# One single chunk and five pairs in each feed-forward in place of three and four, and a one-row bias table

## The chip, the cores and the metric

One NeuronCore of one Trainium2 chip runs the whole program. The metric is device time in microseconds, the median of three runs. Engines are named as in the profile: PE (TensorE), DVE (VectorE), ACT (ScalarE), POOL (GpSimd) and SP (SyncE); SP and POOL issue most transfers.

## The reference

All sizes: 256 tokens, width 1024, float32. The first block has two layers. Layer 0 is a Conformer convolution, layer 1 a causal differential attention of 8 heads with a T5 relative bias. Behind each stands the feed-forward and a gated projection of side features. A second block of three branches follows. What the change touches:

```python
def swiglu(x, w_gate, w_up, w_down):
    return (jax.nn.silu(x @ w_gate) * (x @ w_up)) @ w_down      # width 2816

u = rms_norm(h, ffn_norm_g[i])                                  # once a layer
h = h + swiglu(u, ffn_w_gate[i], ffn_w_up[i], ffn_w_down[i])

bias = jnp.transpose(rel_bias[t5_bucket(dist)], (2, 0, 1))      # dist = q_pos - k_pos
logits = jnp.where(dist >= 0, logits + bias, -jnp.inf)
```

## The kernel before, in words

**Arithmetic.** Each float32 matrix product is made of three passes of reduced-precision matmuls: with x_hi and w_hi, x_lo and w_hi, x_hi and w_lo. `w_hi` is a rounded copy of a weight piece, made by ACT (`feed`, line 1297), and `w_lo` what is left of it, made by DVE (`feed`, line 1857), of a few pieces by POOL (line 1069). A weight piece is 128 x 2048 numbers, 1 MB. PE needs w_hi from the first pass and w_lo from the third.

**Stream.** All weights form one list of operations (`STREAM`, `FFN_ORDER`). Each takes its place in three slots of `w_hi` and `w_lo` in turn, so that w_hi of an operation can be made when PE has left the one three places back (`w_used`). SP loads the plain pieces in the order of the list into four buffers `raw` (line 385) and asks for one when w_lo of the piece four back has been made.

**Feed-forward.** The gate and up columns are cut in 11 chunks of 256 and 256. A *single* chunk is two operations of 24 matmuls (`token_chunk`, line 441). A *pair* of chunks is computed by Strassen's scheme in Winograd's form: with tokens and depth halved, seven products of 12 matmuls (`product`, line 564) in place of eight. B11, B21 and B22 use plain weight pieces. T1, T2, T3 and T4 use sums of pieces, kept in three slots `sums` in the arena. POOL's queue loads them and adds to them by accumulating transfers: T1 is a load of B11 (line 1164, for the first pair 1115) and an accumulation of B12 (line 1106). T4 is a load of B12 (line 1168, first pair 1150) and an accumulation of B22 (line 1109). T2 is T1 + B22, added by DVE (line 1994, `second_sum`). T3 is an accumulation of B21 upon T2 (line 1156). The sums of the tokens' side (`q_hi`, `q_lo`) are made once a layer by DVE and ACT while chunk 0 runs.

Out of the products p1 to p7 come four quarters: chunk one or two, tokens 0 or 1. ACT copies three of them out of PSUM (`c_11`, `c_22`, `c_12`), DVE adds the others, ACT takes the silu and DVE multiplies (`gated`, lines 1361 and 1979). The semaphore `hidden` counts the quarters in the order of `MADE`. A finished hidden chunk is transposed by PE (`hidden_job`, line 603) and split by ACT and DVE (lines 1353 and 1972). Then a *down* operation (24 matmuls) adds its product to four banks. The order of PE, of ACT's and DVE's work and of the queues is written out by hand: a down piece and the transposing of another chunk lie between the products of a pair.

**Bias.** A row of 384 numbers for each head, with the distance falling, is written to DRAM 128 times for each head (line 1177), and read back with a row step of 383, which shifts each partition by one (lines 1181 and 1183). `masked` (line 2267) adds it to the logits.

## Time and profile before

| | |
|---|---|
| median of three runs | 1002.41 us (1000.92 to 1003.13) |
| the profiled execution's own time | 1003.63 us |
| its span | 1001.6 us |
| PE busy | 988.1 us (99%) |
| DVE, ACT, POOL busy | 775.3, 609.2, 153.6 us |
| DMA | 242.01 MB, 242 GB/s over the span |
| SP's queue q1, POOL's queue q0 | 43.8% and 28.2% of the sixteen engines' span |

A matmul's end is modelled and the next one starts before it, so what one costs is read from the starts. The feed-forwards lie from 109.7 us to 288 us and from 429.4 us to 605 us.

### The profile page before, as it was taken

Reading aid. Unit: us, or ns where it says so; the run is one execution under the profiler, and the core shown is the slowest. Engines: PE = TensorE matmul, PEld = TensorE weight load, DVE = VectorE, ACT = ScalarE, POOL = GpSimd, SP = SyncE. Lnnn points to the kernel's source line nnn. Section 1 sums busy time; section 2 is a strip of 40 time slices with the busy share of each in tenths; the row PEclk is TensorE's granted clock in tenths of the full one; section 3 lists DMA queues with packets and bytes.
Section 4 is the critical chain, followed back from the end, with each engine's and each line's share of the span. In section 5 each row is a group of like instructions: output and inputs, shape, how many; then the busy total and the mean of one; then the engine's idle time right before and its main releaser. Section 6 shows DMA issues by size and latency. Waiting matters only on the chain.

```text
span 1001.6 us, 13597 instructions
## 1 busy us (share of the span) xinstructions
PE 988.1 (99%) x5350; PEld 835.5 (83%) x5350; DVE 775.3 (77%) x909; ACT 609.2 (61%) x722; POOL 153.6 (15%) x150
## 2 busy tenths in 40 slices
PE   8999999999999999999999999999999999999997
PEld 8977888888778888788888888788888889999886
DVE  6996888879567666787988857876877788777874
ACT  6437567657376668666676646754857574444733
POOL 4992101101030320111111002100100010000000
PEclk9999999999999999999999999999999999999999
DMA  8862899999784632779999864577789898545631
GB/s 324 256 217 90 274 298 324 334 300 305 209 292 161 238 128 85 256 264 300 331 343 338 256 218 167 189 256 280 262 258 341 237 311 299 186 169 179 220 126 43
DMA packets 37726, 242.01 MB, mean 242 GB/s; under 512 B 4504, under 2 KB 7064, under 8 KB 9760
## 3 DMA queue, kind: packets, MB, share of 16 engines
q1 hardware_dynamic: 23904, 167.26, 43.8%
q0 software_dynamic: 10736, 70.71, 28.2%
q10 hardware_dynamic: 3024, 3.18, 1.3%
q8 instruction: 43, 0.70, 0.3%
q14 instruction: 19, 0.16, 0.0%
HBM read 237.91 MB, written 3.21 MB: 241 GB/s over the span
## 4 chain that ended last, share of the span: by engine, by line
PE 80%; DVE 8%; DMA 6%; issue 3%; ACT 1%; POOL 0%; SPq 0%; ACTq 0%; POOLq 0%; DVEq 0%
PE bank L441 45%; PE bank L564 18%; DVE bank L2160 4%; PE bank L427 4%; PE bank L429 4%; PE bank L428 4%; DMA raw<-in_ws 4%; DMA arena<-in_ws 3%; PE bank L478 2%; DVE w_lo L1857 2%; PE bank L603 1%; PE bank L847 0%; DMA u_scr<-arena 0%; PE bank L944 0%; PE bank L977 0%
## 5 line engine op out<-in xcount | busy, mean ns | idle before, releaser
L1857 DVE TENSOR_TENSOR w_lo<-raw,w_hi 128x2048 fp32r<-128x2048 f32 x145 | 332.8, 2303 | 84.0 <-ACT w_hi L1297 83.7
L1297 ACT ACTIVATE w_hi<-raw 128x2048 fp32r<-128x2048 f32 x156 | 298.2, 1912 | 107.9 <-PE bank L441 71.3
L1297 ACT ACTIVATE w_hi<-arena 128x2048 fp32r<-128x2048 f32 x48 | 92.4, 1924 | 57.2 <-PE bank L441 21.0
L441 PE MATMUL bank<-w_hi,x_hi 128*128 128x512 f32 x416 | 115.0, 398 | 0.2
L1857 DVE TENSOR_TENSOR w_lo<-arena,w_hi 128x2048 fp32r<-128x2048 f32 x48 | 109.2, 2285 | 5.3 <-ACT w_hi L1297 5.2
L441 PE MATMUL bank<-w_lo,x_hi 128*128 128x512 f32 x416 | 111.5, 390 | 0.0
L441 PE MATMUL bank<-w_hi,x_lo 128*128 128x512 f32 x416 | 111.5, 390 | 0.0
L441 PE MATMUL bank<-w_hi,z_hi 128*128 128x512 f32 x320 | 94.2, 394 | 0.3 <-DVE z_lo L1972 0.3
L441 PE MATMUL bank<-w_lo,z_hi 128*128 128x512 f32 x320 | 92.9, 390 | 0.1
L441 PE MATMUL bank<-w_hi,z_lo 128*128 128x512 f32 x320 | 92.9, 390 | 0.0
L441 PEld LDWEIGHTS bank<-w_hi,x_lo 128*128 128x128 f32 x416 | 78.1, 188 | 16.8
L441 PEld LDWEIGHTS bank<-w_lo,x_hi 128*128 128x128 f32 x416 | 78.1, 188 | 16.5
L441 PEld LDWEIGHTS bank<-w_hi,x_hi 128*128 128x128 f32 x416 | 75.2, 188 | 16.3 <-issue 1.7
L428 PE MATMUL bank<-x_lo,w_hi 128*128 128x256 f32 x256 | 72.4, 283 | 0.0
L429 PE MATMUL bank<-x_hi,w_lo 128*128 128x256 f32 x256 | 72.4, 283 | 0.0
L427 PE MATMUL bank<-x_hi,w_hi 128*128 128x256 f32 x256 | 72.4, 283 | 0.0
L441 PEld LDWEIGHTS bank<-w_lo,z_hi 128*128 128x128 f32 x320 | 60.0, 188 | 13.1 <-DVE w_lo L1857 0.5
L441 PEld LDWEIGHTS bank<-w_hi,z_lo 128*128 128x128 f32 x320 | 60.1, 188 | 12.7
L441 PEld LDWEIGHTS bank<-w_hi,z_hi 128*128 128x128 f32 x320 | 58.8, 188 | 12.5 <-DVE z_lo L1972 0.7
L1069 POOL TENSOR_TENSOR w_lo<-raw,w_hi 128x2048 fp32r<-128x2048 f32 x11 | 50.7, 4615 | 110.9 <-ACT w_hi L1297 110.8
L564 PE MATMUL bank<-w_hi,q_hi 128*128 128x512 f32 x192 | 52.9, 397 | 1.0 <-ACT arena L1751 1.0
L564 PE MATMUL bank<-w_lo,q_hi 128*128 128x512 f32 x192 | 51.6, 391 | 0.0
(292 smaller groups left out, 1592.3 us busy)
## 6 DMA issues: line engine op xcount, KB each, us to landing
raw<-in_ws SPq DMA_DIRECT2D x156, 1024.0 KB, 7.3
arena<-in_ws POOLq DMA_DIRECT2D x60, 1024.0 KB, 11.4
arena<-u_scr ACTq DMA_DIRECT2D x16, 142.0 KB, 4.9
arena<-in_rows POOLq DMA_DIRECT2D x2, 1024.0 KB, 6.6
toep<-bias_row POOLq DMA_DIRECT2D x1, 1536.0 KB, 44.7
h<-in_x_tok SPq DMA_DIRECT2D x2, 512.0 KB, 4.0
raw<-in_ws SPq DMA_DIRECT2D x2, 512.0 KB, 8.0
arena<-in_rows POOLq DMA_DIRECT2D x2, 512.0 KB, 7.5
```

The costliest lines, as they stand in the source:

```text
L427: pe.matmul(dst, s_hi, m_hi, start=first, stop=False)
L428: pe.matmul(dst, s_hi, m_lo, start=False, stop=False)
L429: return pe.matmul(dst, s_lo, m_hi, start=False, stop=last)
L441: ins = pe.matmul(dst, tok(a_part, k, t), w_part[:, s, c], start=first and j == 0 and i == 0, stop=last and j == 2 and i == len(ks) - 1)
L478: ins = pe.transpose(banks[b][:, k * P:(k + 1) * P], src[:, k * P:(k + 1) * P], ident[:, :])
L564: ins = pe.matmul(banks[b][:, :], a_part[:, k, :], w_part[:, o % SPLIT, k * 512:(k + 1) * 512], start=start and j == 0 and k == 0, stop=j ...
L603: ins = pe.transpose(banks[t_bank][:, k * SEQ + t * P:k * SEQ + (t + 1) * P], hids[i % 3][:, t, k * P:(k + 1) * P], ident[:, :])
L1069: pool.tensor_tensor(w_lo[:, g % SPLIT, :], operand(g), w_hi[:, g % SPLIT, :].bitcast(F32), ALU.subtract).then_inc(S("lo_pool"), 1)
L1297: act.activation(w_hi[:, g % SPLIT, :], operand(g), ACT.Copy).then_inc(hi_done, 1)
L1857: dve.tensor_tensor(w_lo[:, g % SPLIT, :], operand(g), w_hi[:, g % SPLIT, :].bitcast(F32), ALU.subtract).then_inc(lo_done, 1)
L2160: ins = dve.scalar_tensor_tensor(out=y_odd[:, f % 2, :] if tap == TAPS - 2 else sums[c], in0=shifted, scalar=w, in1=sums[c], op0=ALU.mult, ...
```

## The change

Chunk 1 and chunk 10, single before, become part of pairs: (1, 2), (3, 4), (5, 6), (7, 8), (9, 10) behind the single chunk 0. B21 moves to the second place of a pair. The first and the last pair have one down piece within them, behind T4; the others have two. Three down pieces (7, 10, 9) stand at the end of a layer. The quarter (one, 0) is gated first, before T2's turn is over, and DVE gates the last quarter before it makes w_lo of the next pair. POOL's queue adds T3 of the first pair before it loads T1 of the second. PE's banks alternate between two arrangements. The bias row has the distance rising and is written once for each head, 383 numbers; one load reads it with a step of one number from partition to partition, and `masked` reads it backwards.

```diff
-STEPS = (0, 1, (2, 3), (4, 5), (6, 7), (8, 9), 10)
-PAIRS = [s for s in STEPS if isinstance(s, tuple)]
+STEPS = (0, (1, 2), (3, 4), (5, 6), (7, 8), (9, 10))
+PAIRS = STEPS[1:]
 NPAIR = len(PAIRS)
-WITHIN = {(2, 3): (0, 1), (4, 5): (3, 2), (6, 7): (5, 4), (8, 9): (7, 6)}
-BEHIND = {10: (9, 8, 10)}
-
-TURNED = {(2, 3): (1, None), (4, 5): (3, 2), (6, 7): (5, 4), (8, 9): (7, 6), 1: (0,), 10: (9,)}
-LAST_DOWN = BEHIND[10][-1]
-
-FFN_ORDER = []
-for _step in STEPS:
-    if isinstance(_step, tuple):
-        FFN_ORDER += [(_step, "B11"), (_step, "T1"), (_step, "T2"), (_step, "B22"), ("down", WITHIN[_step][0]),
-                      (_step, "B21"), (_step, "T4"), ("down", WITHIN[_step][1]), (_step, "T3")]
-    else:
-        FFN_ORDER += [("gu", _step, 0), ("gu", _step, 1)] + [("down", i) for i in BEHIND.get(_step, ())]
+WITHIN = {(1, 2): (0,), (3, 4): (2, 1), (5, 6): (4, 3), (7, 8): (6, 5), (9, 10): (8,)}
+BEHIND = (7, 10, 9)
+
+TURNED = {(1, 2): (None, 0), (3, 4): (2, 1), (5, 6): (4, 3), (7, 8): (6, 5), (9, 10): (8, 7)}
+LAST_DOWN = BEHIND[-1]
+
+FFN_ORDER = [("gu", 0, 0), ("gu", 0, 1)]
+for _p in PAIRS:
+    FFN_ORDER += [(_p, "B11"), (_p, "B21"), (_p, "T1"), (_p, "T2"), (_p, "B22")]
+    FFN_ORDER += [("down", i) for i in WITHIN[_p][:-1]] + [(_p, "T4"), ("down", WITHIN[_p][-1]), (_p, "T3")]
+FFN_ORDER += [("down", i) for i in BEHIND]
...
 for _layer in range(2):
-    for _step in STEPS:
-        if isinstance(_step, tuple):
-            MADE += [(_layer, _step[1], 0), (_layer, _step[0], 0), (_layer, _step[1], 1), (_layer, _step[0], 1)]
-        else:
-            MADE += [(_layer, _step, t) for t in range(TT)]
+    MADE += [(_layer, 0, t) for t in range(TT)]
+    for _one, _two in PAIRS:
+        MADE += [(_layer, _one, 0), (_layer, _two, 0), (_layer, _two, 1), (_layer, _one, 1)]
...
                     one, two = p
                     n = pair_no(layer, p)
-                    b1, b4, b2 = [(1 + PAIRS.index(p) + j) % 3 for j in range(3)]
+                    b1, b4, b2 = ((2, 1, 0), (1, 2, 0))[PAIRS.index(p) % 2]
                     turned, within = TURNED[p], WITHIN[p]
                     product(("p1", n), ffn_at(layer, p, "B11"), *of_x(0, t0), b1, True, (S("c_11"), 2 * n - 1))
-                    hidden_job(turned[0])
-                    if n == NPAIR * layer + 1:
+                    if turned[0] is not None:
+                        hidden_job(turned[0])
+                    product(("p2", n), ffn_at(layer, p, "B21"), *of_x(1, t0), b2, True, (S("c_11"), 2 * n))
+                    if p == PAIRS[0]:
                         pe.wait_ge(S("q_lo"), layer + 1)
                     product(("p5", n), ffn_at(layer, p, "T1"), *of_q(0), b4, True, (S("c_22"), 2 * n - 1))
                     product(("p6", n), ffn_at(layer, p, "T2"), *of_q(1), b1, False, (S("c_12"), 2 * n - 1))
-                    if turned[1] is not None:
-                        hidden_job(turned[1])
+                    for i in turned[1:]:
+                        hidden_job(i)
                     product(("p3", n), ffn_at(layer, p, "B22"), *of_q(2), b4, False, (S("c_12"), 2 * n))
-                    down(within[0])
-                    product(("p2", n), ffn_at(layer, p, "B21"), *of_x(1, t0), b2, True, (S("c_11"), 2 * n))
+                    for i in within[:-1]:
+                        down(i)
                     product(("p7", n), ffn_at(layer, p, "T4"), *of_q(3), b1, False, (S("c_22"), 2 * n))
-                    down(within[1])
+                    down(within[-1])
                     product(("p4", n), ffn_at(layer, p, "T3"), *of_x(1, t1), b1, False, (S("hidden"), MADE_NO[layer, one, 1]))
-                for step in STEPS:
-                    if isinstance(step, tuple):
-                        pair(step)
-                    else:
-                        single(step)
+                token_chunk(("gu", layer, 0), g0, x_hi, x_lo, ready=ready_from(m),
+                            release=lambda t: (S("hidden"), MADE_NO[layer, 0, t]), hooks=later(m, 1))
+                for p in PAIRS:
+                    pair(p)
+                for j, i in enumerate(BEHIND):
+                    if j + 1 < len(BEHIND):
+                        hidden_job(BEHIND[j + 1])
+                    down(i)
             def ple(layer, m):
                 g0 = G[f"ple{layer}"]
...
                 for before, p in zip(PAIRS, PAIRS[1:]):
                     lo_ready(pool, ffn_at(layer, before, "T1"))
                     sum_there(pool, layer, before, "T2")
+                    if before == PAIRS[0]:
+                        third_sum(layer, before)
                     pool.dma_start(sums[:, 0, :], ws[PIECE_OF[ffn_at(layer, p, "B11")]]).then_inc(S("t1_in"), 16)
-                    third_sum(layer, before)
+                    if before != PAIRS[0]:
+                        third_sum(layer, before)
                     second_part("T1", layer, p)
                     lo_ready(pool, ffn_at(layer, before, "T4"))
                     pool.dma_start(sums[:, 2, :], ws[B12_ROW[layer, p]]).then_inc(S("t4_in"), 16)
@@ -1174,14 +1165,11 @@
             weight_sums(0)
             pool.wait_ge(S("bias_row"), 1)
             pool.wait_ge(S("bias_masked"), 1)
-            pool.dma_start(toep, bias_row[:, :].unsqueeze(1).to_broadcast([HEADS, P, 384])).then_inc(S("toep_out"), 16)
+            pool.dma_start(toep, bias_row[:, 0:383]).then_inc(S("toep_out"), 16)
             low(G["ple0"] + 1)
             h_factor(1)
             pool.wait_ge(S("toep_out"), 16)
-            pool.dma_start(toep_t[:, :, 0:SEQ], bass.AP(toep.tensor, P - 1, [[383, P], [P * 384, HEADS], [1, SEQ]])) \
-                .then_inc(S("ld_toep"), 16)
-            pool.dma_start(toep_t[:, :, SEQ:384], bass.AP(toep.tensor, 2 * P - 1, [[383, P], [P * 384, HEADS], [1, P]])) \
-                .then_inc(S("ld_toep"), 16)
+            pool.dma_start(toep_t, bass.AP(toep.tensor, 0, [[1, P], [383, HEADS], [1, SEQ]])).then_inc(S("ld_toep"), 16)
...
+                def first():
+
+                    ahead(g0)
+                    act.wait_ge(S("r_done"), m + 1)
                     for t in range(TT):
-                        bank, _ = take(act, (("gu", layer, i), t))
-                        gated(i, t, bank[:, 0:256])
-                        if i == 0 and t == 0:
+                        bank, _ = take(act, (("gu", layer, 0), t))
+                        gated(0, t, bank[:, 0:256])
+                        if t == 0:
                             act.wait_ge(S("q_sums"), layer + 1)
                             act.activation(q_hi.rearrange("p i k c -> p (i k c)"),
                                            q_f32.rearrange("p i k c -> p (i k c)"), ACT.Copy).then_inc(S("q_hi"), 1)
-                            ahead(g + 1)
-                    behind = BEHIND.get(i, ())
-                    for j, k in enumerate(behind):
-                        if j + 1 < len(behind):
-                            hidden_hi(behind[j + 1])
-                        ahead(ffn_at(layer, "down", k))
+                            ahead(g0 + 1)
...
-                    ahead(o)
                     while left:
                         left.pop()()
+                    ahead(o)
                     bank, _ = take(act, ("p1", n))
                     act.activation(c_11, bank[:, :], ACT.Copy).then_inc(S("c_11"), 1)
                     ahead(o + 1)
-                    hidden_hi(turned[0])
+                    if turned[0] is not None:
+                        hidden_hi(turned[0])
+                    ahead(o + 2)
+                    act.wait_ge(S("c_11"), 2 * n)
+                    gated(one, 0, c_11[:, 0:256])
                     bank, _ = take(act, ("p5", n))
                     act.activation(c_22, bank[:, :], ACT.Copy).then_inc(S("c_22"), 1)
-                    ahead(o + 2)
-                    if turned[1] is not None:
-                        hidden_hi(turned[1])
+                    ahead(o + 3)
+                    for i in turned[1:]:
+                        hidden_hi(i)
                     bank, _ = take(act, ("p6", n))
                     act.activation(c_12, bank[:, :], ACT.Copy).then_inc(S("c_12"), 1)
-                    ahead(o + 3)
                     ahead(o + 4)
+                    ahead(o + 5)
                     act.wait_ge(S("c_12"), 2 * n)
                     gated(two, 0, c_12[:, 0:256])
-                    ahead(o + 5)
-                    ahead(o + 6)
-                    act.wait_ge(S("c_11"), 2 * n)
-                    gated(one, 0, c_11[:, 0:256])
+                    ahead(ffn_at(layer, p, "T4"))
                     act.wait_ge(S("c_22"), 2 * n)
                     gated(two, 1, c_22[:, 0:256])
-                    ahead(o + 7)
-                    ahead(o + 8)
+                    ahead(ffn_at(layer, p, "T3"))
...
-                for step in STEPS:
-                    if isinstance(step, tuple):
-                        pair(step)
-                    else:
-                        single(step)
+                first()
+                for p in PAIRS:
+                    pair(p)
+                left.pop()()
+                for j, i in enumerate(BEHIND):
+                    if j + 1 < len(BEHIND):
+                        hidden_hi(BEHIND[j + 1])
+                    ahead(ffn_at(layer, "down", i))
...
+                def first():
+
+                    feed(g0 + 1)
+                    input_sums(m)
+                    ahead(g0)
...
+                        if t == 0:
                             input_lo(m)
-                            ahead(g + 1)
-                    behind = BEHIND.get(i, ())
-                    for j, k in enumerate(behind):
-                        if j + 1 < len(behind):
-                            hidden_lo(behind[j + 1])
-                        ahead(ffn_at(layer, "down", k))
+                            ahead(g0 + 1)
+                    second_sum(PAIRS[0])
                 def pair(p):
                     one, two = p
                     n, o = pair_no(layer, p), ffn_at(layer, p, "B11")
                     turned = TURNED[p]
-                    ahead(o)
                     while left:
                         left.pop()()
-                    hidden_lo(turned[0])
+                    ahead(o)
+                    if turned[0] is not None:
+                        hidden_lo(turned[0])
                     ahead(o + 1)
+                    p_2, _ = take(dve, ("p2", n))
+                    dve.wait_ge(S("c_11"), 2 * n - 1)
+                    dve.tensor_tensor(c_11, p_2[:, :], c_11, ALU.add).then_inc(S("c_11"), 1)
                     ahead(o + 2)
-                    if turned[1] is not None:
-                        hidden_lo(turned[1])
+                    dve.wait_ge(S("c_11"), 2 * n)
+                    gated(one, 0, c_11[:, 256:512])
+                    for i in turned[1:]:
+                        hidden_lo(i)
+                    ahead(o + 3)
                     p_53, _ = take(dve, ("p3", n))
                     dve.wait_ge(S("c_12"), 2 * n - 1)
                     dve.tensor_tensor(c_12, p_53[:, :], c_12, ALU.subtract).then_inc(S("c_12"), 1)
-                    ahead(o + 3)
+                    ahead(o + 4)
                     dve.wait_ge(S("c_12"), 2 * n)
                     gated(two, 0, c_12[:, 256:512])
-                    ahead(o + 4)
-                    ahead(o + 5)
-                    p_2, _ = take(dve, ("p2", n))
-                    dve.wait_ge(S("c_11"), 2 * n - 1)
-                    dve.tensor_tensor(c_11, p_2[:, :], c_11, ALU.add).then_inc(S("c_11"), 1)
+                    ahead(ffn_at(layer, p, "T4") - 1)
                     u_3, _ = take(dve, ("p7", n))
                     dve.wait_ge(S("c_22"), 2 * n - 1)
                     dve.tensor_tensor(c_22, c_22, u_3[:, :], ALU.subtract).then_inc(S("c_22"), 1)
-                    dve.wait_ge(S("c_11"), 2 * n)
-                    gated(one, 0, c_11[:, 256:512])
-                    ahead(o + 6)
+                    ahead(ffn_at(layer, p, "T4"))
                     dve.wait_ge(S("c_22"), 2 * n)
                     gated(two, 1, c_22[:, 256:512])
-                    ahead(o + 7)
+                    ahead(ffn_at(layer, p, "T3"))
                     if p != PAIRS[-1]:
                         second_sum(PAIRS[PAIRS.index(p) + 1])
-                    ahead(o + 8)
...
+                first()
+                for p in PAIRS:
+                    pair(p)
+                left.pop()()
+                for j, i in enumerate(BEHIND):
+                    if j + 1 < len(BEHIND):
+                        hidden_lo(BEHIND[j + 1])
+                    ahead(ffn_at(layer, "down", i))
...
-            act.activation(bias_row[:, 0:SEQ], bank[0:HEADS, 0:SEQ], ACT.Copy).then_inc(S("bias_row"), 1)
+            act.activation(bias_row[:, P - 1:P - 1 + SEQ], bank[0:HEADS, 0:SEQ], ACT.Copy).then_inc(S("bias_row"), 1)
...
-            pool.memset(bias_row[:, SEQ:384], NEG).then_inc(S("bias_masked"), 1)
+            pool.memset(bias_row[:, 0:P - 1], NEG).then_inc(S("bias_masked"), 1)
...
-                        ins = dve.tensor_tensor_reduce(v[:, lo:lo + w], bank[:, k0:k0 + w], toep_t[:, hd, k0:k0 + w],
+                        ins = dve.tensor_tensor_reduce(v[:, lo:lo + w], bank[:, k0:k0 + w], toep_t[:, hd, w - 1::-1] if w < SEQ else toep_t[:, hd, ::-1],
...
-            dve.wait_ge(S("ld_toep"), 32)
+            dve.wait_ge(S("ld_toep"), 16)
...
-    dist = np.arange(SEQ - 1, -1, -1)
+    dist = np.arange(SEQ)
...
-    toep = nc.dram_tensor("toep", (HEADS, P, 384), F32).ap()
+    toep = nc.dram_tensor("toep", (HEADS, 383), F32).ap()
```

## Rows read from the trace of the kernel before

**Rows 1.** The page: busy time, share and instructions; DMA share in 40 slices.

```profile
PE 988.1 (99%) x5350; PEld 835.5 (83%) x5350; DVE 775.3 (77%) x909; ACT 609.2 (61%) x722; POOL 153.6 (15%) x150
...
DMA  8862899999784632779999864577789898545631
```

**Rows 2.** Waits of PE: line, releaser, us in total, times, longest.

```profile
PE bank L603 <- DVE z_lo L1972: 1.0, 1, 1.0
```

**Rows 3.** Windows: length, busy time of each engine, clock, DMA share, GB/s.

```profile
109.60:132.80 23.20, 23.20 (x110) 19.27 (x109) 22.12 (x19) 12.91 (x13) 3.84 (x5) 1.00 0.83 274
...
191.40:222.40 31.00, 31.00 (x143) 25.61 (x142) 24.40 (x18) 20.91 (x18) 3.71 (x5) 1.00 1.03 318
...
510.60:541.50 30.90, 30.90 (x142) 25.54 (x141) 26.91 (x20) 21.20 (x18) 3.62 (x5) 1.00 1.02 324
```

**Rows 4.** Windows of 5 us: accumulating pieces alone, then plain ones alone.

```profile
140.00:145.00 5.00, 5.00 (x24) 4.14 (x23) 4.43 (x3) 4.31 (x4) 0.86 (x1) 1.00 0.92 192
...
235.00:240.00 5.00, 4.93 (x22) 3.72 (x21) 5.00 (x5) 4.29 (x5) 0.00 (x0) 1.00 1.02 203
155.00:160.00 5.00, 5.00 (x24) 4.14 (x23) 4.69 (x5) 2.63 (x3) 0.00 (x0) 1.00 1.00 424
475.00:480.00 5.00, 5.00 (x24) 4.13 (x23) 5.00 (x5) 2.32 (x2) 0.00 (x0) 1.00 1.02 429
```

**Rows 5.** Timeline of PE (start us, us): chunk 0's end, T2, B22, two pairs' starts.

```profile
121.47 1.07 PE L441 MATMUL bank<-w_hi,x_hi 128*128 128x512 f32 x4
...
138.79 1.07 PE L564 MATMUL bank<-w_hi,q_hi 128*128 128x512 f32 x4
...
141.51 1.07 PE L564 MATMUL bank<-w_hi,q_hi 128*128 128x512 f32 x4
...
163.27 1.07 PE L564 MATMUL bank<-w_hi,x_hi 128*128 128x512 f32 x4
...
194.19 0.62 PE L564 MATMUL bank<-w_hi,x_hi 128*128 128x512 f32 x2
```

**Rows 6.** Timeline of DVE: behind chunk 0 in layer 0, a sum of quarters, layer 1.

```profile
125.74 0.48 DVE L1979 SCALAR_TENSOR_TENSOR arena<-bank,st,arena 128x256 f32<-128x256 f32 x1
126.14 2.28 DVE L1994 TENSOR_TENSOR arena<-arena,raw 128x2048 f32<-128x2048 f32 x1
128.34 2.28 DVE L1857 TENSOR_TENSOR w_lo<-raw,w_hi 128x2048 fp32r<-128x2048 f32 x1
...
144.43 0.69 DVE L2038 TENSOR_TENSOR arena<-bank,arena 128x512 f32<-128x512 f32 x1 [0.57 <-PE bank L564]
...
448.02 2.28 DVE L1857 TENSOR_TENSOR w_lo<-raw,w_hi 128x2048 fp32r<-128x2048 f32 x1
```

**Rows 7.** Timeline of POOL (first load of T4) and ACT (w_hi of T3, T4, T4).

```profile
118.67 0.64 POOL L1150 DMA_DIRECT2D arena<-in_ws  x1 [4.77 <-DVE arena L1956]
...
438.38 0.62 POOL L1150 DMA_DIRECT2D arena<-in_ws  x1 [4.78 <-DVE arena L1956]
...
218.04 1.92 ACT L1297 ACTIVATE w_hi<-arena 128x2048 fp32r<-128x2048 f32 x1 [4.36 <-DMA arena<-in_ws]
...
238.82 1.93 ACT L1297 ACTIVATE w_hi<-arena 128x2048 fp32r<-128x2048 f32 x1 [0.71 <-DMA arena<-in_ws]
...
557.39 1.93 ACT L1297 ACTIVATE w_hi<-arena 128x2048 fp32r<-128x2048 f32 x1 [0.42 <-DMA arena<-in_ws]
```

**Rows 8.** T1(8,9): w_lo, third pass; bias table: transfer, ACT's waits behind it, reductions.

```profile
227.87 4.49 DVE L1857 TENSOR_TENSOR w_lo<-arena,w_hi 128x2048 fp32r<-128x2048 f32 x2
...
230.21 1.20 PE L564 MATMUL bank<-w_lo,q_hi 128*128 128x512 f32 x4
...
toep<-bias_row POOLq DMA_DIRECT2D x1, 1536.0 KB, 44.7
...
ACT w_hi L1297 <- DMA raw<-in_ws: 18.1, 6, 5.3
...
L2267 DVE CUSTOM_DVE_ANT_0 arena<-bank,arena 128x256 f32<-128x256 f32 x16 | 6.7, 421 | 5.6 <-PE bank L848 5.5
```

47 lines of the change are left out of this document (3 added, 44 removed).

## The prediction

> **What bounds the kernel now.** I read the page's busy shares and slices first. TensorE is busy 988.1 us of a 1001.6 us span, 99% [rows 1]. Next the waits of TensorE: few, and the largest in a feed-forward is 1.0 us, once, in layer 0: the transposes of a hidden chunk wait for VectorE's z_lo [rows 2]. So a TensorE instruction taken away is worth its full price, as long as its feeders stay ahead. Then I read the DMA line of the page: it reaches 9 exactly in the two feed-forwards (and in stretches of the second block). Cut at the starts of pairs, the sixteen DMA engines are full there: share 1.03 and 318 GB/s in the third pair of layer 0, 1.02 and 324 GB/s in that of layer 1, while the stretch over chunks 0 and 1 has 0.83 [rows 3]. The kernel is thus at two limits at once in the pairs, TensorE and the DMA engines, and the second one is hidden only by work that was fetched ahead.
>
> How close is shown by ScalarE, which makes w_hi from what arrives: in layer 0 it waits 4.36 us for T3 of the third pair and 0.71 us for T4 of the fourth (arena: the POOL queue's sums) [rows 7]. It gets away with it because w_hi is made up to three operations ahead. But TensorE's third pass of T1(8,9), which needs w_lo, starts at 230.21; w_lo was ready at 227.87 + 2.28 = 230.15, so the slack is gone [rows 6, 8]. (Which operation a w_hi or w_lo row belongs to is counted by its place in the stream.)
>
> **The change: TensorE.** Twelve matmuls make one product: T2 starts at 138.79 and B22 at 141.51, 2.72 us [rows 5]. One half of a single chunk and a down piece have 24 matmuls of the same shape each, 5.44 us. Two single chunks (10.88 us each) become one pair of seven products (19.04 us): 2.72 us saved a layer, 5.44 us in all. Transposes and down pieces keep their number.
>
> **The first pair, VectorE.** Up to the second sum VectorE does the same as before in the same order, and it is full (22.1 of 23.2 us, [rows 3]): gating 125.74, second sum 126.14, next w_lo 128.34 to 130.62 [rows 6]. Before, that last one was B11's. Now it is T1's, and TensorE, which starts B11 at 121.47, B21 at 124.19 and T1 at 126.91, wants it at the third pass, 126.91 + 1.81 = 128.72 (a pass is 0.91 us, [rows 5]). Stall 1.9 us. Layer 1 is the same 319.7 us later (w_lo 448.02) [rows 6]. Counting on with durations of [rows 6] (w_lo 2.28, gating 0.48, and 0.69 for c_11, c_12 and z_lo, all of 512 columns), w_lo of down 0 is ready at 130.62 + 2.28 + 0.69 + 2.28 + 0.48 + 0.69 + 2.28 + 0.69 + 2.28 = 142.3; TensorE, with T1's delay, would want it at 141.2. That is 3.0 us of stall at least, since VectorE must not idle once; with 0.9 us of idling behind ScalarE's T4 and z_hi it is 3.9 us. This alone eats the 2.72 us of the layer.
>
> **The DMA engines.** This is the large term. A plain piece of 1.05 MB: where only plain pieces move, the engines give 424 to 429 GB/s, so 2.46 us of all sixteen. An accumulating one: where nothing else moves, 192 to 203 GB/s, so 5.3 us [rows 4]. A pair with two down pieces moves seven plain ones (three B pieces and two down on SP's queue, two loads on POOL's) and three accumulating ones: 7 x 2.46 + 3 x 5.3 = 33.1 us, against TensorE's 194.19 - 163.27 = 30.92 us [rows 5]. Each such pair thus eats about 2 us of what was fetched ahead. Two single chunks need four plain pieces, 9.8 us, for 21.8 us of TensorE: they were the rest in which the engines caught up. A pair needs eight, three of them accumulating, 28.2 us for 19.04 us.
>
> I test the prices on the old kernel. From the issue of T4's first load (118.67) to the arrival of T4(8,9) (ScalarE starts on it at 238.82, just released by DMA) are 120.1 us; in layer 1 557.39 - 438.38 = 119.0 us [rows 7]. By the code, in that time POOL's queue lands 17 pieces (10 accumulating) and SP's 18: 25 x 2.46 + 10 x 5.3 = 114.5 us. The rest, 5 us, is idling at the start. Now the same stretch up to T4(9,10): POOL's queue lands 22 (13 accumulating), SP's 18 to 22, I take 21. 30 x 2.46 + 13 x 5.3 + 5 = 147.7 us, so T4 arrives at 118.67 + 147.7 = 266.4. TensorE starts an operation 2.4 us behind its data at the earliest (1.93 w_hi, 2.28 w_lo, less the 1.81 us to the third pass) [rows 5 to 7]. It would be there without any stall at 121.47 + 25.0 (first pair: seven products, one down piece, a transposing of 0.5, which is half of 30.92 - 19.04 - 10.88) + 3 x 30.92 + 14.6 (five products and two transposings) = 253.8, because the last pair has one down piece ahead of T4 fewer. 266.4 + 2.4 - 253.8 = 15.0 us. This holds the stalls of VectorE, which come earlier in the same layer. The engines have nothing accumulating but one T3 sum after that, so it isn't given back. Layer 1: arrival 438.38 + 147.7 = 586.1, wanted 253.8 + 319.7 = 573.5, again 15.0. Net 15.0 - 2.7 = 12.3 us a layer, 24.6 us.
> Ends of this term: no idling and SP's 18 pieces give 135.3 us and 2.6 us, below VectorE's 3.0, so 0.3 us net a layer; 5.5 us for an accumulating piece, 8 us of idling and SP's 22 give 156 us, a stall of 23 us, 20 net.
>
> At this place the Trainium skill speaks against me. "DMA: Bandwidth & Descriptors", section "Measured", gives 341 GB/s for a transfer of 1 MB and names no extra price for accumulating. By it ten pieces take 10.49 MB / 341 = 30.8 us, just under TensorE's 30.92, and the engines would keep up. Our trace differs on both sides: 424 GB/s plain, 192 accumulating. The page's "Issuing engines are not separate DMA queues" agrees with shares that stop at 1.03 for SP's and POOL's queues together [rows 3]; it means that moving pieces between the queues buys nothing.
>
> **Order of the queues.** In the first pair T3's sum goes ahead of T1's next load on POOL's queue. Both have to pass anyway; T3 gets there in time (its price 5.3 us of engine time, asked for at 133, used at 146) and the next T1 is later by one transfer: 0 to 3 us within the 15. The gating of (one, 0) now comes before p5's copy on ScalarE and B22 on TensorE waits for that copy; by the times above it is free at 134.7, B22 would start at 134.8: nothing.
>
> **The bias table.** The write of 1536 KB took 44.7 us and lay on the engines from 233 to 278; raw pieces behind it were late, 18.1 us of ScalarE's waits, and TensorE lost the 1.0 us of [rows 2] in this stretch [rows 8]. The write becomes 12 KB: that 1.0 us returns. The single read of 1024 KB in place of 1024 and 512 is hidden (nobody waited). The reductions that read the table backwards are 16 of 421 ns and 16 of half that width [rows 8]; the trace shows no backward read. If it costs nothing, 0; if double, some 11 us of VectorE, spread over attention, where it waits 5.5 us for the logits alone: 0 to +2 us. I take 0, the nearest row being the same instruction forwards.
>
> **Sum.** -5.4 + 30.0 - 1.0 = +23.6 us on the profiled execution's own 1003.63 us (span 1001.6, 2.0 around it): 1027.2. Against the median, 1002.41, which is 1.2 lower, it is 1026.0; rounded down to 1025, since SP's pieces may be fewer than 21.
>
> **Rivals.** *VectorE's first pair alone* (the engines keep up). In rows: the engines would move ten pieces in less than TensorE's 30.92 us. For it: TensorE had no stall of this kind in four pairs, though the share was 1.02. Against it: the waits that grow from pair to pair [rows 7]. Then 2 x (3.9 + 0 to 2.5 for the next T1 - 2.72) - 1.0 = +1 to +6: 1004 to 1009. This is the way in which the page quoted above would have it.
> *It pays* (the other side): VectorE's queue of the first pair is caught up, since TensorE's wait at T1 moves down 0's too, and the engines deliver T4(9,10) before it is wanted. The point that decides is the arrival of T4(9,10): by 251.4 (253.8 - 2.4) there is no stall. That needs 132.7 us for 43 pieces, 15 less than my count, below even the low end. Time: 1002.4 - 5.4 - 1.0 = 996.0.
> *The bias table is all one sees*: stalls of VectorE's least, 3 us a layer, against the 2.7 saved, and -1.0: 1002.0, within 0.2%.
> *Worse than the sum*: each wait for data makes a gap in which nothing is fetched, since raw pieces are asked for only when w_lo is made. The share would fall under 1 in the pairs. 23 us of stall a layer: 1041.
>
> **Chances.** DMA engines bind (1014 to 1034): 0.70. VectorE alone (1004 to 1009, and what lies between): 0.13. Worse than the sum: 0.05. Bias table alone, same: 0.04. It pays: 0.08. The range is 1005 to 1034; the likeliest one's own is 1014 to 1034. Within 0.2% (2 us) can't be told from no change here. Faster 0.08, same 0.05, slower 0.87.
>
> **What would show it.** Right: TensorE waits for w_hi or w_lo at T4 and T1 of the later pairs, ScalarE for "arena<-in_ws" with tens of microseconds in each layer; DMA share 1.0 from the first to the fifth pair; T4(9,10) arriving near 266 and 586 plus layer 0's shift; a stall of about 1.9 us at the first T1 of each layer; the write of the table gone, and with it the wait of 1.0 us of the transposes for z_lo at the end of layer 0. Wrong: DMA share under 0.95 in the pairs with TensorE at full (the count of engine time fails), more than 345 GB/s over a pair, or a longer feed-forward whose waits are for VectorE with the data there.

## The result and the profile after

The changed kernel takes 1034.57 us (median of 6 runs, 1029.25 to 1037.25), the kernel before 1002.71 us beside it (6 runs, 1000.92 to 1004.34). The ratio is 1.0309, 95% interval 1.0289 to 1.0330. The profiled execution took 1033.34 us, its span is 1031.5 us, so 29.9 us of span more. The forecast's range ended at 1034: the profiled execution lies just inside it, the median of the six 0.6 us outside.

| | before | after |
|---|---|---|
| feed-forward of layer 0, first to last matmul | 109.67 to 288.2 | 109.54 to 301.8 |
| feed-forward of layer 1 | 429.39 to 605.5 | 442.91 to 635.4 |
| lengths | 178.6, 176.1 us | 192.2, 192.5 us |
| from one to the other | 141.2 us | 141.1 us |

All of the 30 us lies in the two feed-forwards: 13.7 and 16.4 us. The page of after, to set beside [rows 1]:

```profile
PE 994.8 (96%) x5326; PEld 830.6 (81%) x5326; DVE 796.0 (77%) x923; ACT 621.0 (60%) x734; POOL 160.0 (16%) x159
...
DMA  8863899999765533689999976469598979554631
```

TensorE runs 24 matmuls fewer. In the page its waits are in the lines of the pairs (line, releaser, us in total, times, longest), where [rows 2] had one of 1.0 us:

```profile
PE bank L437 <- DVE w_lo L1836: 8.4, 9, 1.3
PE bank L560 <- ACT arena L1389: 6.0, 3, 2.9
PE bank L560 <- DVE w_lo L1836: 4.8, 7, 1.8
PE bank L560 <- DVE arena L1958: 4.8, 5, 2.1
```

L437 is the matmul of a down piece, L560 that of a product. ScalarE's own waits in the two feed-forwards (100 to 310 us, then 430 to 640 us) are for the sums on POOL's queue, 78.2 us in all:

```profile
ACT w_hi L1285 <- DMA arena<-in_ws: 38.6, 11, 8.4
```
```profile
ACT w_hi L1285 <- DMA arena<-in_ws: 39.6, 12, 8.2
```

In the kernel before they are 18.0 us (100 to 310 us, then 425 to 610 us):

```profile
ACT w_hi L1297 <- DMA arena<-in_ws: 13.1, 6, 4.4
```
```profile
ACT w_hi L1297 <- DMA arena<-in_ws: 4.9, 3, 2.7
```

Windows (columns as in [rows 3]) from the second pair on, and timelines of TensorE, then of ScalarE: the first T1 (130.56) and T4(9,10) (270.74, and 604.37 in layer 1), the places that the prediction named, and T1(3,4) (158.91):

```profile
158.90:192.00 33.10, 32.47 (x136) 25.56 (x137) 25.43 (x18) 20.28 (x18) 3.71 (x5) 0.95 1.01 313
192.00:224.00 32.00, 30.28 (x133) 23.72 (x132) 27.02 (x20) 20.41 (x18) 3.70 (x5) 1.00 1.02 320
224.00:256.00 32.00, 31.28 (x143) 25.53 (x142) 26.27 (x20) 21.21 (x19) 3.70 (x5) 1.00 1.02 323
```
```profile
130.56 1.20 PE L560 MATMUL bank<-w_lo,q_hi 128*128 128x512 f32 x4 [1.76 <-DVE w_lo L1836]
...
158.91 1.16 PE L560 MATMUL bank<-w_hi,q_hi 128*128 128x512 f32 x4 [2.14 <-DVE arena L1958]
...
161.20 1.91 PE L560 MATMUL bank<-w_lo,q_hi 128*128 128x512 f32 x4
162.90 1.03 PE L560 MATMUL bank<-w_hi,q_hi 128*128 128x512 f32 x2
...
270.74 1.17 PE L560 MATMUL bank<-w_hi,q_hi 128*128 128x512 f32 x4 [2.93 <-ACT arena L1389]
...
604.37 2.04 PE L560 MATMUL bank<-w_hi,q_hi 128*128 128x512 f32 x4 [2.69 <-ACT arena L1389]
```
```profile
267.71 1.91 ACT L1285 ACTIVATE w_hi<-arena 128x2048 fp32r<-128x2048 f32 x1 [3.05 <-DMA arena<-in_ws]
269.52 0.58 ACT L1341 ACTIVATE z_hi<-bank 128x512 fp32r<-128x512 f32 x1
```

T4(9,10) is started by ScalarE at 267.71 and by TensorE at 270.74; without any stall TensorE would be there at 253.7 (the prediction's 253.8, less the 0.13 us by which this feed-forward starts sooner). So 17.0 us have been lost by then. What is named there is ScalarE's copy at L1389, not a transfer: the copy stood in ScalarE's queue behind a w_hi that waited 3.05 us for its sum. The wait has to be followed one engine further to find the transfer.

### The profile page after: what moved, and what is told of

It is laid out like the page before. It is cut to its first block, busy times and chain, and to the rows that moved or that the text cites. A ratio compares the mean times of both kernels' runs of the same rounds, so it can differ in the third digit from the quotient of the medians.

```text
span 1031.5 us, 13610 instructions
## 1 busy us (share of the span) xinstructions
PE 994.8 (96%) x5326; PEld 830.6 (81%) x5326; DVE 796.0 (77%) x923; ACT 621.0 (60%) x734; POOL 160.0 (16%) x159
## 3 DMA queue, kind: packets, MB, share of 16 engines
q0 software_dynamic: 11360, 79.10, 30.3%
## 4 chain that ended last, share of the span: by engine, by line
PE 67%; DVE 12%; DMA 11%; issue 6%; ACT 3%; POOL 1%; POOLq 0%; DVEq 0%; ACTq 0%
PE bank L437 40%; PE bank L560 12%; DMA arena<-in_ws 10%; DVE w_lo L1836 4%; DVE bank L2128 4%; PE bank L423 4%; PE bank L425 4%; PE bank L424 4%; PE bank L474 2%; DVE arena L1973 1%; PE bank L674 1%; PE bank L835 0%; DMA u_scr<-arena 0%; DVE q_lo L1941 0%; ACT x_hi L1312 0%
## 5 line engine op out<-in xcount | busy, mean ns | idle before, releaser
L1285 ACT ACTIVATE w_hi<-arena 128x2048 fp32r<-128x2048 f32 x56 | 107.6, 1922 | 113.6 <-DMA arena<-in_ws 78.2
L1836 DVE TENSOR_TENSOR w_lo<-arena,w_hi 128x2048 fp32r<-128x2048 f32 x56 | 127.8, 2284 | 22.2 <-ACT w_hi L1285 22.0
L437 PE MATMUL bank<-w_lo,z_hi 128*128 128x512 f32 x320 | 94.0, 393 | 8.4 <-DVE w_lo L1836 8.4
L437 PE MATMUL bank<-w_hi,x_hi 128*128 128x512 f32 x352 | 97.5, 399 | 0.2
L437 PE MATMUL bank<-w_hi,z_hi 128*128 128x512 f32 x320 | 94.3, 394 | 0.1
L437 PE MATMUL bank<-w_hi,x_lo 128*128 128x512 f32 x352 | 94.3, 390 | 0.0
L437 PE MATMUL bank<-w_lo,x_hi 128*128 128x512 f32 x352 | 94.3, 390 | 0.0
L437 PE MATMUL bank<-w_hi,z_lo 128*128 128x512 f32 x320 | 92.9, 390 | 0.0
L437 PEld LDWEIGHTS bank<-w_lo,z_hi 128*128 128x128 f32 x320 | 59.3, 188 | 24.3 <-DVE w_lo L1836 12.4
L437 PEld LDWEIGHTS bank<-w_hi,x_lo 128*128 128x128 f32 x352 | 66.1, 188 | 14.3
L437 PEld LDWEIGHTS bank<-w_lo,x_hi 128*128 128x128 f32 x352 | 66.1, 188 | 13.9
L560 PE MATMUL bank<-w_hi,q_hi 128*128 128x512 f32 x224 | 63.1, 404 | 12.2 <-ACT arena L1389 6.0
L437 PEld LDWEIGHTS bank<-w_hi,x_hi 128*128 128x128 f32 x352 | 63.5, 188 | 14.1 <-issue 1.7
L437 PEld LDWEIGHTS bank<-w_hi,z_lo 128*128 128x128 f32 x320 | 60.1, 188 | 12.9
L437 PEld LDWEIGHTS bank<-w_hi,z_hi 128*128 128x128 f32 x320 | 58.9, 188 | 12.2 <-issue 0.7
L560 PE MATMUL bank<-w_lo,q_hi 128*128 128x512 f32 x224 | 62.4, 401 | 4.5 <-DVE w_lo L1836 4.4
```

Source lines behind the costliest of these rows:

```text
L437: ins = pe.matmul(dst, tok(a_part, k, t), w_part[:, s, c], start=first and j == 0 and i == 0, stop=last and j == 2 and i == len(ks) - 1)
L560: ins = pe.matmul(banks[b][:, :], a_part[:, k, :], w_part[:, o % SPLIT, k * 512:(k + 1) * 512], start=start and j == 0 and k == 0, stop=j ...
L1285: act.activation(w_hi[:, g % SPLIT, :], operand(g), ACT.Copy).then_inc(hi_done, 1)
L1836: dve.tensor_tensor(w_lo[:, g % SPLIT, :], operand(g), w_hi[:, g % SPLIT, :].bitcast(F32), ALU.subtract).then_inc(lo_done, 1)
```

## The experiments

Each was timed beside the kernel before; ratios are to it.

**Making the accumulating transfers plain (e1_plain).**

```diff
-   ws[B12_ROW[layer, p]], accum_op=ALU.add).then_inc(S("t1_in"), 16)
+   ws[B12_ROW[layer, p]]).then_inc(S("t1_in"), 16)     # T4's and T3's likewise
```

> The changed kernel with the accumulating transfers of the feed-forwards made plain loads of the same pieces (the second load overwrites the first, so T1, T3 and T4 are not sums: the products that use them are not the reference's). Bytes, queues, waits and all engines' instructions are the same. Theory DMA (the sixteen engines bind, because an accumulating piece costs 5.3 us of them and a plain one 2.46): ten pieces of a pair cost 24.6 us against 30.9 of TensorE, the waits behind the first pair go, what is left is VectorE's 3 us in the first pair of each layer, so 1.000 to 1.007 of the kernel before; DMA share in the pairs about 0.8. Theory VectorE (its queue order binds): nothing changes, 1.025 or more.

Measured: 1012.0 us, ratio 1.0074 (1.0059 to 1.0090), span 1009.4. That is just above the range expected. Three quarters of the loss go with the accumulation, at the same bytes. The share of the DMA engines over a pair falls from 1.02 at 320 to 0.88 at 330 GB/s, not to the 0.8 expected:

```profile
191.00:223.00 32.00, 31.29 (x142) 25.53 (x141) 26.93 (x20) 21.02 (x18) 2.67 (x6) 1.00 0.88 330
```

The queues one by one (packets, MB, share of the sixteen engines), in the changed kernel from 192 to 224 us and in this run from 191 to 223 us, about five pieces each:

```profile
q0 software_dynamic: 716, 5.22, 64.5%
q1 hardware_dynamic: 688, 5.00, 37.6%
```
```profile
q0 software_dynamic: 725, 5.28, 45.4%
q1 hardware_dynamic: 720, 5.24, 42.1%
```

So, as an estimate, a plain piece costs 2.9 us of the engines on POOL's queue and 2.5 to 2.7 on SP's in this mix, and an accumulating one 5.0: the prediction's 2.46 and 5.3 had been read where each kind moves alone.

The rest is VectorE's, on every pair. Its timeline, and TensorE's beside it (one down piece, of which the third pass is late):

```profile
194.71 0.69 DVE L1951 TENSOR_TENSOR z_lo<-bank,z_hi 128x512 fp32r<-128x512 f32 x1 [0.83 <-ACT z_hi L1341]
195.32 2.28 DVE L1836 TENSOR_TENSOR w_lo<-raw,w_hi 128x2048 fp32r<-128x2048 f32 x1
```
```profile
195.88 0.62 PE L437 MATMUL bank<-w_hi,z_hi 128*128 128x512 f32 x2
...
197.66 0.74 PE L437 MATMUL bank<-w_lo,z_hi 128*128 128x512 f32 x2 [0.71 <-DVE w_lo L1836]
...
202.36 0.84 PE L560 MATMUL bank<-w_hi,q_hi 128*128 128x512 f32 x3
```

The down piece takes 202.36 - 195.88 = 6.48 us from start to start, against 5.44 without a wait: 1.04 us for 0.71 us of idle. This stall costs 0.33 us beyond what the page shows as idle; where there is no wait each matmul starts before the one ahead has ended, and at a wait that overlap is missing. With that price for every wait the books of layer 1 close: 176.1 us before, - 2.72, + 5.4 idle in 7 waits, + 7 x 0.33 = 181.1; measured 431.32 to 612.4, 181.1.

**The same on the kernel before (e7_before_plain).**

> The kernel before with its feed-forwards' accumulating transfers made into plain loads (T1, T3 and T4 are then not sums): the counterpart of the changed kernel with all plain. Theory (in the kernel before the engines never bind TensorE, its only wait in a feed-forward is 1.0 us): ratio 0.998 to 1.001. Rival (accumulating transfers also slow TensorE, ScalarE or VectorE down through their traffic in SBUF): faster by 3 us or more, ratio under 0.997, with shorter w_lo or matmul durations.

Measured: 1008.94 us, ratio 1.0052 (1.0034 to 1.0070). Slower, which neither expected. In layer 1 the feed-forward is 176.1 us, to 0.1 as before, and a pair 30.92: accumulation costs TensorE nothing there, as said. The loss lies elsewhere: 2.4 us ahead of the first feed-forward, where the code is the same (a wait for GpSimd's w_lo that the profiled executions of e6_t3_plain and e11_no_sum have too and the others not), and 3.5 us in layer 0, at chunk 10. The write of the 1536 KB bias table was issued at 232.99 us, against 233.33 before, while TensorE was 2.4 us further behind, and the raw pieces of chunk 10 came late (TensorE's timeline, then ScalarE's waits from 225 to 300 us):

```profile
260.77 1.19 PE L441 MATMUL bank<-w_hi,x_hi 128*128 128x512 f32 x4 [2.21 <-ACT w_hi L1297]
```
```profile
ACT w_hi L1297 <- DMA raw<-in_ws: 14.9, 3, 7.1
```

That the write did this is argued and not shown by a run of its own; it fits that e1_plain, where the write has 12 KB, has no such loss in layer 0 (181.2 us, and 181.1 in layer 1). If so, a faster queue moved a transfer to where it did harm.

**Only T3 plain (e6_t3_plain).**

> The changed kernel with only T3's ten accumulating transfers (five a layer) made into plain loads of the same piece, so T3 is not a sum; T1 and T4 still accumulate. A full pair then has eight plain and two accumulating pieces: 8 x 2.46 + 2 x 5.3 = 30.3 us of engine time, just under TensorE's 30.92. Theory (a threshold: the engines cost only what exceeds TensorE's time): T4(9,10) arrives 4 x 2.84 = 11.4 us earlier, nearly as if all were plain, and the time is 0 to 4 us above the 1012.0 us of the run with all plain: ratio 1.006 to 1.012. Rival (each accumulating transfer costs its own share wherever it stands, 23 us over 28 of them in pairs and first pairs): ten of some 28 give back about 8 us, ratio 1.021 to 1.025.

Measured: 1022.95 us, ratio 1.0196 (1.0170 to 1.0222). The threshold expectation falls. The other, an equal price for each transfer, is nearer: its range starts at 1.021, within the interval. The feed-forwards take 187.0 and 186.7 us, so of the 22.4 us that all thirty plain transfers give back in them these ten give 11.1. From the third pair on the stalls are as in the all-plain run, but TensorE still waits 2.35 us at T4(9,10). POOL's queue and ScalarE there:

```profile
237.88 0.54 POOL L1159 DMA_DIRECT2D arena<-in_ws  x1 [0.44 <-DVE w_lo L1836]
253.81 0.89 POOL L1097 DMA_DIRECT2D arena<-in_ws  x1 [15.38 <-DMA arena<-in_ws]
```
```profile
264.52 1.91 ACT L1285 ACTIVATE w_hi<-arena 128x2048 fp32r<-128x2048 f32 x1 [3.04 <-DMA arena<-in_ws]
```

T4's slot comes free at 237.9 (w_lo of the previous T4), the load lands 15.9 us later, the sum is issued and lands at 264.5: 26.6 us in sequence, beside other transfers. The last pair has one down piece fewer ahead of T4, so TensorE wants the next T4 after some 25 us. This chain is no cause beside full engines: while it runs, their share is 0.98 in both halves. The queues over the pair before (191 to 222 us) show what the threshold had wrong:

```profile
237.90:253.80 15.90, 15.90 (x74) 13.19 (x73) 11.74 (x8) 8.88 (x7) 0.53 (x1) 1.00 0.98 337
253.80:264.50 10.70, 10.70 (x50) 8.80 (x49) 9.24 (x8) 5.37 (x6) 1.98 (x3) 1.00 0.98 272
```
```profile
q0 software_dynamic: 721, 5.24, 58.0%
q1 hardware_dynamic: 764, 5.49, 44.6%
```

Scaled to five pieces on each queue that is 18.0 and 13.2 us, 31.2 in all, where 30.3 had been counted and TensorE has 30.92: with only T3 plain the engines are still full.

**The bias table alone, on the kernel before (e2_table).**

```diff
-   pool.dma_start(toep, bias_row[:, :].unsqueeze(1).to_broadcast([HEADS, P, 384]))
+   pool.dma_start(toep, bias_row[:, 0:383])     # one load back, masked reads it backwards
```

> The kernel before with the bias table's part of the change alone. By the prediction the 1.0 us wait at the end of layer 0 goes: 0.998 to 1.000 of the kernel before, and the reductions that read backwards keep their 421 ns. Rival: reading backwards doubles them, some 11 us more of VectorE in attention, 1.001 to 1.003.

Measured: 1002.38 us (7 runs), ratio 0.9979 (0.9964 to 0.9995). Layer 0's feed-forward is 177.4 us, 1.2 less. The stretch between the feed-forwards is 141.1 us, and the reductions that read backwards take 422 ns where [rows 8] have 421:

```profile
L2235 DVE CUSTOM_DVE_ANT_0 arena<-bank,arena 128x256 f32<-128x256 f32 x16 | 6.7, 422 | 5.6 <-PE bank L836 5.5
```
```profile
toep<-bias_row POOLq DMA_DIRECT2D x1, 12.0 KB, 11.1
```

(Both rows are of the changed kernel.) This is the only version here below the kernel before.

**GpSimd relieves VectorE in the first pair (e4_b21_pool).** w_lo of B21 is made by GpSimd between T4's load and its sum.

```diff
-POOL_LO = (*range(2, 11), G["ple0"] + 1, G["ple1"] + 1)
+POOL_LO = (*range(2, 11), ffn_at(0, PAIRS[0], "B21"), G["ple0"] + 1, ffn_at(1, PAIRS[0], "B21"), G["ple1"] + 1)
```

> The changed kernel with w_lo of the first pair's B21 made by GpSimd between T4's load and its accumulation, and w_hi of B21 made before q_hi: VectorE is relieved of 2.3 us at the point where it is late, no transfer moves. Theory DMA: the first pair's stall shrinks by 1 to 3 us a layer, but T4(9,10) arrives when it did (near 267.7), so the time stays within 2 us of the changed kernel, 1.028 to 1.033 of the kernel before. Theory VectorE: 4 to 6 us come back, 1.024 to 1.027.

Measured: 1035.35 us, ratio 1.0305 (1.0291 to 1.0319), as the changed kernel. It is no clean test of VectorE's part, though. GpSimd's w_lo and VectorE's q_lo ran together, and q_lo, 2.29 us in the changed kernel, took 5.88 (timelines of VectorE and GpSimd):

```profile
121.14 5.88 DVE L1941 TENSOR_TENSOR q_lo<-arena,q_hi 128x2048 fp32r<-128x2048 f32 x1 [0.36 <-ACT q_hi L1364]
```
```profile
119.13 5.74 POOL L1057 TENSOR_TENSOR w_lo<-raw,w_hi 128x2048 fp32r<-128x2048 f32 x1
```

**Taking the first second sum from VectorE (e11_no_sum, e12_no_sum_plain).** The two runs that are clean.

```diff
+   w = 64 if p == PAIRS[0] else HALF
-   dve.tensor_tensor(sums[:, 1, :], sums[:, 0, :], raw[:, g % RAW, :], ALU.add)
+   dve.tensor_tensor(sums[:, 1, 0:w], sums[:, 0, 0:w], raw[:, g % RAW, 0:w], ALU.add)
```

> The changed kernel in which VectorE's second sum of the first pair of each layer (2.28 us, T2 = T1 + B22) is made over 64 of 2048 columns only, so T2 of that pair isn't a sum; all transfers stay. VectorE then makes w_lo of the first T1 2.2 us earlier, in time. Theory of the prediction (the stall up to T4(9,10) is set by the arrival of its sum and holds VectorE's stalls, which come earlier in the layer): the wait of 1.8 us at the first T1 goes and comes back at a later wait for a transfer; ratio 1.028 to 1.031, as the changed kernel. Rival (the two stalls add): 2 x 3.2 to 3.6 us less, ratio 1.023 to 1.025.

> The same with all accumulating transfers of the feed-forwards made into plain loads (T1, T3 and T4 are not sums either), to set beside the all-plain run (ratio 1.0074). There no transfer is waited for, so VectorE's first pair is on the path by itself. Theory: T1's wait (1.8 us of idle, 2.1 from start to start), T4's 0.2 and down 0's 0.7 (1.0) go in both layers: 5 to 7 us less, ratio 1.000 to 1.003. Rival (VectorE catches up nothing, each piece is just late by less): 2 to 4 us less, ratio 1.003 to 1.006.

Measured: 1031.72 us, ratio 1.0276 (1.0249 to 1.0303), and all plain 1007.99 us, 1.0062 (1.0038 to 1.0087). With plain transfers the wait of 1.8 us at T1 is gone and the layers are 179.4 and 179.1 us, 1.8 and 2.0 less: just T1's stall, while T4's and down 0's stay. So VectorE catches up nothing (the rival, though the median lies just above its range). With accumulating transfers layer 0 stays the same (191.9 for 192.2 us), T1's wait comes back as 2.33 us at T4(1,2) behind ScalarE; layer 1 wins 3.1 us. So "held in the transfers' stall" holds in one layer and not in the other, in one execution; in layer 0 TensorE's granted clock fell once more than in the changed kernel's (right behind that wait), and the interval reaches both expectations.

**The queue order of the first pair undone (e5_order).**

```diff
-                    if before == PAIRS[0]:
-                        third_sum(layer, before)
                     pool.dma_start(sums[:, 0, :], ws[PIECE_OF[ffn_at(layer, p, "B11")]]).then_inc(S("t1_in"), 16)
-                    if before != PAIRS[0]:
-                        third_sum(layer, before)
+                    third_sum(layer, before)
```

> The changed kernel with one thing undone: in the first pair of each layer POOL's queue loads B11 for T1 of the second pair before it accumulates T3 of the first, as in the other pairs. Bytes and kinds of transfers are the same. Theory (the sixteen DMA engines are full up to T4(9,10), so only the sum of engine time counts, not the order): unchanged against the changed kernel, ratio to the kernel before 1.029 to 1.033. Rival (the order itself costs: T1(3,4) came late by one accumulating transfer, TensorE waited 2.14 us for it in layer 0, and the granted clock fell right behind that wait): 2 to 4 us a layer come back, ratio 1.022 to 1.027, and the wait at T1(3,4) is gone from the trace.

Measured: 1032.02 us, ratio 1.0290 (1.0252 to 1.0328). The wait at T1(3,4) is gone in layer 0, and the time with it isn't: no gain that can be told. T3's sum now comes later, and TensorE waits at T3(1,2) instead, in both layers:

```profile
PE bank L560 <- DVE arena L2014: 3.7, 2, 1.9
```

So the order moved the stall and wasn't seen to make it; the interval reaches into the rival's range, and a gain of 2 us a layer isn't ruled out. The granted clock fell four times in the feed-forwards of this execution, twice in the changed kernel's, three times in e9_last_pair's, and each fall costs some 1.6 us (see below), so a difference of 3 us between such versions can come from the clock alone.

**The last pair with two down pieces inside (e9_last_pair).**

```diff
-WITHIN = {..., (9, 10): (8,)}
-BEHIND = (7, 10, 9)
+WITHIN = {..., (9, 10): (8, 7)}
+BEHIND = (10, 9)
```

> The changed kernel with only the last pair altered: it has two down pieces inside as the other pairs (8 ahead of T4, 7 behind it), and 10 and 9 stand at the end of the layer, so T4(9,10) is wanted one down piece (5.44 us) later; 10's hidden chunk is then transposed right before its down piece, which leaves some 1.3 us of z_hi and z_lo (0.57 + 0.69 us) open. Theory (what bound the changed kernel up to T4(9,10) is the arrival of T4's sum there, 3 us behind ScalarE in layer 0; transfers are the limit and TensorE's work before that point is what counts): the wait for w_hi at T4(9,10) goes, 2 to 3 us a layer, less the 1.3 us at the end: ratio 1.026 to 1.030. Rival (the stalls are made in the pairs before, not at T4(9,10)): no gain, 1.3 us a layer more, ratio 1.032 to 1.035. Rival (all of the down piece's 5.44 us comes back): ratio 1.020 to 1.024.

Measured: 1029.58 us, ratio 1.0239 (1.0204 to 1.0274). The wait of TensorE at T4(9,10) is gone; at the end there is a new one, 2.2 us in each layer, before the transposes can use their bank:

```profile
PE bank L599 <- DVE z_lo L1953: 4.4, 2, 2.2
```

The median is 5 us under the changed kernel's (7 by the ratios), so the last pair's shortened lead cost some 2.5 to 3.5 us a layer net. By the ratio that is just beyond the first expectation and in the range of the last, all of the down piece's 5.44 us; the interval reaches both. In the profiled execution layer 0 is unchanged (192.3 us) and layer 1 has 2.4 us less.

**T3's sum off the queue: GpSimd (e3_t3_pool), VectorE (e8_t3_dve), VectorE earlier (e10_t3_early).** The sum is made from the piece in `raw`, so B21 isn't transferred twice.

```diff
-   pool.dma_start(sums[:, 1, :], ws[PIECE_OF[ffn_at(layer, p, "B21")]], accum_op=ALU.add)
+   loaded(pool, g)                                   # e8, e10: dve, in its own order
+   pool.tensor_tensor(sums[:, 1, :], sums[:, 1, :], raw[:, g % RAW, :], ALU.add)
# SP: the raw buffer of B21 is free only when the sum is made
```

> The changed kernel with T3's sum made by GpSimd (T2 plus the raw piece B21, some 4.6 us of an engine that is 16% busy) in place of the accumulating transfer, and behind the load of the next T1 in the first pair too. Theory DMA: a pair moves seven plain and two accumulating pieces, 17.2 + 10.6 = 27.8 us under TensorE's 30.9, so most of the stall goes: 1.000 to 1.010 of the kernel before. Theory VectorE: 1.025 or more, since VectorE's work is the same.

> The changed kernel with T3's sum made by VectorE (2.28 us each, from B21's piece that is already in raw, so B21 isn't transferred twice) and with z_lo made behind the next w_lo in every pair. A full pair then moves seven plain and two accumulating pieces: 7 x 2.46 + 2 x 5.3 = 27.8 us against TensorE's 30.92. Theory (the DMA engines bind the changed kernel, and what the all-plain run had left, 1012.0 us, is VectorE late by 0.7 us at ten w_lo, each costing TensorE 1.05 us from start to start because the pipeline drains): no waits for transfers; the waits behind B22 go with z_lo's move (VectorE makes that w_lo 1.5 us earlier), 8 of them, 8.4 us; the first pair's 1.8 us at T1 and 0.7 at down 0 stay. 1003 to 1006, ratio 0.999 to 1.004. Rival (VectorE is too full in a pair for 2.28 us more): its w_lo for the down piece behind T4 gets late, 1 to 2 us a pair, ratio 1.008 to 1.018. Rival (B21's raw buffer, held until the sum is made, delays SP's next pieces): waits of ScalarE for raw, ratio over 1.01.

> The changed kernel with the last pair altered as in the run beside it; T3's sum made by VectorE in all pairs but the first, right behind the w_lo of the down piece that follows B22 and not behind the gating as in the run before (1.0518), so that B21's raw buffer is held some 12 us less; z_lo behind that sum. Eight transfers a run fewer, none of them plain. Theory (the run before lost its time because SP could ask for the next pair's B11 only when the sum was made, three raw pieces then came in a bunch, and the DMA engines idled before; VectorE itself has the 2.28 us): the waits of ScalarE for raw shrink from 3 to 4 us a pair to under 1 us; what stays is the first pair's 3.6 us, T4(9,10) without a wait, 1.3 us at the end; ratio 1.001 to 1.010. Rival (VectorE has no room: w_lo of T4 or of the second down piece is late in each pair): 1 to 2 us a pair, ratio 1.010 to 1.020. Rival (holding B21 at all breaks the ring of four raw buffers): ratio over 1.025.

Measured: 1045.63 us, ratio 1.0403 (1.0387 to 1.0419); 1054.30 us, 1.0518 (1.0497 to 1.0540); 1031.39 us, 1.0262 (1.0231 to 1.0294). All missed their first expectation. In e3_t3_pool ScalarE waits for no transfer any more in the feed-forwards, but VectorE's w_lo stands still beside GpSimd's add, in each pair (timelines, then TensorE's waits):

```profile
198.95 6.40 DVE L1836 TENSOR_TENSOR w_lo<-raw,w_hi 128x2048 fp32r<-128x2048 f32 x1
```
```profile
198.52 4.68 POOL L1148 TENSOR_TENSOR arena<-arena,raw 128x2048 f32<-128x2048 f32 x1 [2.09 <-DVE w_lo L1836]
```
```profile
PE bank L562 <- DVE w_lo L1836: 29.6, 13, 2.9
```

In e8_t3_dve the sum takes 2.28 us of VectorE, but B21's buffer is held to the end of it, and ScalarE waits for T3's sum (L1980), for T2's (L1973, 5.8 us in the changed kernel), and for raw pieces that come late in a bunch (100 to 310 us):

```profile
ACT w_hi L1285 <- DVE arena L1980: 20.3, 5, 5.2
ACT w_hi L1285 <- DVE arena L1973: 17.0, 5, 5.0
ACT w_hi L1285 <- DMA raw<-in_ws: 16.8, 7, 3.6
```

TensorE's granted clock fell seven times in the feed-forwards of e3_t3_pool's profiled execution and eight times in e8_t3_dve's, so a part of their loss is the clock's.

In e10_t3_early the sum comes 10.8 us behind the start of T1's w_lo in place of 14.6, and half of the loss is back, with the better last pair in it; the bunching isn't gone (three pieces are asked for within 0.9 us of 203.14). Beside e9_last_pair, which has the same last pair and T3 on the queue, it is no faster (1031.39 and 1029.58 us). So the transfers that VectorE's sum saves gained nothing there: each buffer held in the ring of four delays the pieces behind it, the last expectation of both runs.

## Why the prediction was right, and where its sizes were not

The forecast was +23.6 us on the profiled execution's own 1003.63 us; it is +29.7 (1033.34). Direction, mechanism and place were right; the time is at the upper end of the range. Of the 6 us that the sum is short, 4.3 lie at T4(9,10), 17.0 and 17.3 us late in place of 15.0 twice, and 2.4 behind it; the table gave 0.2 more back.

- *TensorE, -5.4*: right. 24 matmuls fewer, and the books of layer 1 close with 2.72.
- *VectorE's first pair*: first T1 predicted 1.9 us late, measured 1.76 (130.56). The first pair in all, 3.0 to 3.9 predicted, is 3.6 in the all-plain run. But the step was too small: I counted no pair but the first, and put it inside the transfers' stall. In the all-plain run VectorE's lateness is 5.3 and 5.4 us of idle in 6 and 7 waits, with 0.33 for each 7.3 and 7.7 us, of which 4.1 lie at one down piece in each of the later pairs, where z_lo waits 0.83 us for ScalarE and w_lo stands behind it. In that run it is the whole of what is left.
- *The DMA engines, 15.0 a layer*: T4(9,10) arrives at 267.7, predicted 266.4; stall 17.0 by then. 0.6 of the difference is the start behind the data, 3.0 us and not 2.4, since the copy L1389 stood between. Between the runs, accumulation is worth 1031.5 - 1009.4 = 22.1 us of span, 11 a layer. The count of pieces held: from 118.6 to 267.7 us the two queues moved 45.62 MB, 43.5 pieces against 43, at a share of 1.00. The arrival within 1.3 us is in part luck even so. The split of the price was wrong, and errors cancel in the mix of seven and three (33.3 us against 33.1 counted); with T3 alone plain they don't (31.2 against 30.3), and there T4(9,10) came 5.3 us sooner, from the start of the feed-forward, and not 11.4. And the 5 us of idling isn't there; it made up for prices too low in all (POOL's queue 62.8% of the stretch, 93.6 us against 91.0 counted, SP's 36.5%, 54.4 against 51.7). Also, TensorE is late at T4(9,10) in the all-plain run too, by 259.81 - 253.2 = 6.6 us (its feed-forward starts 0.65 us sooner than before's). TensorE there:

```profile
259.81 1.07 PE L560 MATMUL bank<-w_hi,q_hi 128*128 128x512 f32 x4
```

- *Behind T4(9,10)*: "isn't given back" was right; 0.6 and 1.8 us come on top. Not foreseen: TensorE's granted clock fell twice to 1.2 GHz. Around 160 and 604 us the windows read

```profile
160.00:164.00 4.00, 4.00 (x12) 2.96 (x11) 4.00 (x4) 2.61 (x3) 1.43 (x2) 0.57 0.94 297
603.50:608.00 4.50, 3.63 (x10) 2.90 (x11) 4.16 (x4) 2.53 (x3) 0.00 (x0) 0.62 0.81 269
```

  and the third pass of T1(3,4) takes 162.90 - 161.20 = 1.70 us in place of 0.91. In both cases a wait of 2.1 to 2.7 us of TensorE had just ended; but the wait of 2.93 us at 270.74 was followed by no such fall, so a wait doesn't always bring it. In the all-plain run and in the kernel before the clock doesn't fall in the feed-forwards. Each fall cost 1.6 us, by the starts of the passes.
- *Queue order, 0 to 3 us within the 15*: not contradicted (e5_order); the wait that it brought to T1(3,4) is 2.14 us.
- *Gating order, "B22 would start at 134.8: nothing"*: right for the first pair, wrong as a rule. Of after's waits 6.0 us name ScalarE's copy and 4.8 the gating on VectorE. They are the transfers' waits handed on by an in-order queue: in the all-plain run TensorE has neither. So they are no term of their own, but the forecast had them nowhere.
- *Bias table, -1.0, and backward reads 0*: right, -1.2 in layer 0 and 422 against 421 ns.

The sum as measured, on the span: -5.4 (TensorE), +15.0 (VectorE), -1.2 (table) = +8.4, against +7.8 for the all-plain run, whose waits it was read from. The accumulating transfers, with the falls of the clock behind their waits, are what is left, 22.1. Of the rivals, "VectorE alone" is what the all-plain run shows: +7.8 us of span, above its 1 to 6. The Trainium skill, "DMA: Bandwidth & Descriptors", section "Measured", gives 341 GB/s for 1 MB and no price for accumulating; by it all runs should have looked like that one. No run here shows an accumulating transfer at 341 GB/s. The same page of the Trainium skill, section "Issuing engines are not separate DMA queues", says that transfers run on the same 16 engines whichever engine starts them; the share of 1.02 for both queues together agrees.

What stays open: whether full engines could serve T4(9,10) sooner if its load didn't have to wait for the one slot. A run with a second slot for T4 would tell; it wasn't tried. Nor does any run keep the sums and free the engines without holding something else up.

## What to carry to other kernels

When two small steps are fused into one denser step, count what each limit does in the steps that vanish: the single chunks were not only slower on TensorE, they were where VectorE and the DMA engines caught up. Price a stall from start to start, and look at all places with thin slack, not only the first one that turns negative. And before an operation is moved to an idle engine or held in a buffer longer, ask what it then stands beside or holds up: VectorE's instructions beside GpSimd's, or the next pair's loads in the ring of buffers.

## What the runs showed of the hardware

- An accumulating transfer of 1 MB moves at 192 to 203 GB/s alone, plain ones at 424 to 429 [rows 4]; in the mix of a pair it costs an estimated 5.0 us of the sixteen engines, a plain one 2.5 to 2.9. A kernel that differs in nothing else is 22 us faster without accumulation (e1_plain).
- VectorE and GpSimd tensor_tensor on SBUF at once: w_lo 2.28 us alone, 6.40 beside GpSimd's add of 4.68; q_lo 2.29 and 5.88. In both cases VectorE's instruction ends 2.15 us behind GpSimd's (205.35 and 203.20, 127.02 and 124.87), nearly its whole length alone. The kernel before has it too, ahead of the first feed-forward (VectorE, two w_lo in 6.81 us, 2.3 more than two alone; GpSimd beside them):

```profile
93.66 6.81 DVE L1857 TENSOR_TENSOR w_lo<-raw,w_hi 128x2048 fp32r<-128x2048 f32 x2 [1.04 <-ACT w_hi L1297]
```
```profile
93.55 2.56 POOL L1121 TENSOR_TENSOR h<-h,arena 128x512 f32<-128x512 f32 x2
```

  The Trainium skill, "SBUF — State Buffer", section "Who interferes with whom", has the rule: a VectorE instruction with two inputs in SBUF contends with a GpSimd instruction that reads SBUF. The traces agree, with these numbers. I had not weighed it when I moved T3's sum.
- A short wait of TensorE costs some 0.3 us more than its idle time: 1.04 for 0.71 us at a down piece of e1_plain, and 2.04 for 1.76 us at the first T1 of the changed kernel.
